# Eight routed experts in a different order, with a form for 32 tokens and a scatter in four steps

## The reference

```
def _moe(h, router_w, router_b, wg, wu, wd):
    logits = (h @ router_w + router_b).astype(jnp.float32)
    top_v, top_i = lax.top_k(logits, MOE_TOPK)
    top_w = jax.nn.softmax(top_v, axis=-1)
    gates = jnp.sum(top_w[..., None] * jax.nn.one_hot(top_i, N_EXPERTS, dtype=jnp.float32), axis=-2)
    ...
    for e in range(N_EXPERTS):
        out = out + gates[..., e:e + 1] * _swiglu(h, wg[e], wu[e], wd[e])
```

## Time and profile before

| | us |
|---|---|
| median of 3 runs | 2050.29 (2046.76 to 2052.06) |
| the profiled execution | 2052.97 |
| its span in the profile | 2051.2 |
| TensorE busy | 1945.4 (95% of the span) |
| VectorE, ScalarE, GpSimd busy | 501.9, 276.1, 351.3 |
| first product of the experts to the last | 1053.9 to 2028.4 |

### The profile page before, as it was taken

How to read it: one execution, slowest core, us unless ns; L and a number is a source line. 1 busy time by engine, 2 the same in 40 slices (tenths; PEclk the granted TensorE clock), 3 DMA queues, 4 the chain that set the end, 5 groups by cost and what they waited for, 6 DMA issues and landing times.

```text
span 2051.2 us, 28236 instructions
## 1 busy us (share of the span) xinstructions
PE 1945.4 (95%) x11415; PEld 1379.9 (67%) x11416; DVE 501.9 (24%) x1098; ACT 276.1 (13%) x519; POOL 351.3 (17%) x215
## 2 busy tenths in 40 slices
PE   7999799989999999999979999998988999999998
PEld 5888588867776788888855555554446877554444
DVE  1794734110001391434130101110101100101102
ACT  2104212010001203412020001010000000101002
POOL 2609900079993000000000000000000000000000
PEclk9999899999999999999979999999999999999999
DMA  9746433267773343333479999999999666799840
GB/s 381 256 152 226 164 124 122 85 241 258 269 274 147 121 163 131 117 110 123 174 305 401 420 417 352 417 422 422 422 422 420 241 245 246 308 382 421 311 179 22
DMA packets 73841, 533.82 MB, mean 260 GB/s; under 512 B 8320, under 2 KB 8320, under 8 KB 8960
## 3 DMA queue, kind: packets, MB, share of 16 engines
q1 hardware_dynamic: 67680, 489.72, 60.8%
q0 software_dynamic: 5760, 41.95, 5.6%
q10 hardware_dynamic: 288, 0.50, 0.1%
HBM read 531.08 MB, written 1.05 MB: 259 GB/s over the span
## 4 chain that ended last, share of the span: by engine, by line
PE 84%; SPq 4%; DMA 4%; DVE 4%; ACT 2%; issue 2%; POOL 1%; ACTq 0%; DVEq 0%
PE ps L614 21%; PE ps L953 17%; PE ps L988 9%; PE ps L677 7%; PE ps L686 7%; PE ps L1017 6%; SPq L449 4%; PE ps L697 4%; PE ps L1033 3%; PE ps L912 2%; PE ps L929 2%; DMA ring<-in_moe_units 1%; DMA xc<-in_moe_units 1%; DMA proj<-in_ada_units 1%; PE ps L973 1%
## 5 line engine op out<-in xcount | busy, mean ns | idle before, releaser
L614 PE MATMUL ps<-hT,ring 128*128 128x256 f32 x2048 | 454.4, 383 | 5.0 <-ACT hT L1136 5.0
L614 PEld LDWEIGHTS ps<-hT,ring 128*128 128x128 f32 x2048 | 390.9, 192 | 61.0 <-issue 8.3
L953 PE MATMUL ps<-ring,proj 128*64 128x256 f32 (+2 forms) x1768 | 204.7, 369 | 7.9 <-DMA ring<-in_moe_units 7.9
L534 POOL TENSOR_TENSOR aring<-aring,ccol 128x2048 f32<-128x2048 f32 x40 | 145.0, 3624 | 236.6 <-ACT hT L1136 162.8
L953 PEld LDWEIGHTS ps<-ring,proj 128*64 128x64 f32 (+2 forms) x1768 | 119.6, 134 | 86.1 <-issue 41.0
L1663 DVE TENSOR_TENSOR proj<-proj,ps 128x256 f32<-128x256 f32 (+2 forms) x49 | 23.4, 479 | 616.5 <-PE ps L953 616.5
L686 PE MATMUL ps<-hT,ring 128*128 128x256 f32 x704 | 156.8, 385 | 4.0 <-ACT hT L1136 4.0
L686 PEld LDWEIGHTS ps<-hT,ring 128*128 128x128 f32 x704 | 135.4, 194 | 22.5 <-issue 4.4
L540 POOL TENSOR_TENSOR aring<-aring 128x1024 f32<-128x1024 f32 x80 | 149.4, 1867 | 6.3
L1466 DVE SCALAR_TENSOR_TENSOR misc<-cpad,par,misc 128x256 f32<-128x256 f32 x240 | 102.7, 511 | 0.0
L1259 ACT ACTIVATE proj<-ps 128x256 f32<-128x256 f32 (+2 forms) x49 | 21.0, 429 | 590.6 <-PE ps L953 590.6
(11 more groups left out here) (291 smaller groups left out, 2042.0 us busy)
## 6 DMA issues: line engine op xcount, KB each, us to landing
ring<-in_moe_units SPq DMA_DIRECT2D x144, 1024.0 KB, 14.1
ring<-in_dense_units SPq DMA_DIRECT2D x121, 1024.0 KB, 5.0
aring<-in_moe_units SPq DMA_DIRECT2D x48, 1024.0 KB, 12.7
proj<-in_moe_units SPq DMA_DIRECT2D x48, 1024.0 KB, 16.1
aring<-in_ada_units POOLq DMA_DIRECT2D x40, 1024.0 KB, 6.2
extra<-in_moe_units SPq DMA_DIRECT2D x24, 1024.0 KB, 12.8
xc<-in_moe_units SPq DMA_DIRECT2D x24, 1024.0 KB, 16.3
misc<-in_moe_units SPq DMA_DIRECT2D x24, 1024.0 KB, 18.3
```

Source lines behind the costliest of these rows:

```text
L534: last = g.tensor_tensor(w, w, ccol[:, :].unsqueeze(2).broadcast_to([P, KT, 256]), ALU.mult)
L614: last = mm(ps[:, n % 2, j * SEQ:(j + 1) * SEQ], wide(s)[:, k, j * P:(j + 1) * P], hT[:, k, :], start=(k == 0), stop=(k == KT - 1))
L953: last = mm(ps[rows * c:rows * (c + 1), bank, 4 * t0:4 * (t0 + rows)], xg[:, 4 * h + k, t0:t0 + rows], w[:, k, 4 * rows * c:4 * rows * (c ...
```

## The change

1. VectorE ranks experts 1 to 7 by their count on the chip and permutes the counts, `key9` and `gate9` accordingly. With r the rank (0 for most tokens), the place among the seven is min(2r, 13 - 2r). Expert 0 stays first. For the counts above the order is 0, 5, 6, 7, 3, 1, 2, 4, with 24, 153, 20, 128, 30, 67, 41 and 49 tokens.
2. SP reads from the new tensor `turn` which expert's weights to load: it waits for `ord_s`, which VectorE gives when the order is made, before unit 14 of the first expert, and reads two entries at the start of each pass.
3. There is a body for up to 32 tokens (`quarter_rows`). Gate and up products have a 32-token stationary operand in four column quarters, each of which sums two of the eight slices of the width 1024 for all 512 columns. ScalarE and VectorE copy the partial sums out, and `sum_and_turn` adds the four quarters and transposes in one, by products with `stk` (four stacked 32x32 identities). Then come silu on ScalarE, the product on VectorE, and the down product in four quarters.
4. The scatter is done in four steps, in groups 1 to 4, each behind a branch of its own (`by_rows`: 64, 128 or 256 rows). A step makes two of the eight tiles, one in bank 6 and one in bank 7. Up to 64 tokens its two products have 64 rows, one in each row half of the array. In `quarter_rows` the two halves of the inner sum lie in rows 0 to 31 and 32 to 63 and are added by the same product.

```diff
-SIZES = (HALF, 96, 128, 160, 256)
+SIZES = (QUARTER, HALF, 96, 128, 160, 256)
...
+        def by_rows(eng, count, body):
+
+            with eng.If(count <= HALF):
+                body(HALF)
+            with eng.Else():
+                with eng.If(count <= P):
+                    body(P)
+                with eng.Else():
+                    body(SEQ)
+                eng.nop()
+
         def count_after(eng, e):
+            eng.wait_ge(ord_s, 1)
             return eng.value_load(cnt[0:1, ds(e + 2, 1)], min_val=0, max_val=SEQ)
...
                 expert_load(0, u)
+            def expert_of(place):
+                return sp.value_load(turn[0:1, place], min_val=0, max_val=EXPERTS - 1)
+
+            sp.wait_ge(ord_s, 1)
             with sp.Fori(0, EXPERTS - 1) as e:
+                now, following = expert_of(ds(e, 1)), expert_of(ds(e + 1, 1))
                 for u in range(EXP_SLOTS, UNITS):
                     sp.wait_ge(unit_s, e * UNITS + (u - EXP_SLOTS + 1))
-                    expert_load(e, u)
+                    expert_load(now, u)
                 for u in range(EXP_SLOTS):
                     sp.wait_ge(unit_s, e * UNITS + (UNITS + u - EXP_SLOTS + 1))
-                    expert_load(e + 1, u)
+                    expert_load(following, u)
+            final = expert_of(slice(EXPERTS - 1, EXPERTS))
             for u in range(EXP_SLOTS, UNITS):
                 sp.wait_ge(unit_s, (EXPERTS - 1) * UNITS + u - EXP_SLOTS + 1)
-                expert_load(EXPERTS - 1, u)
+                expert_load(final, u)
...
+            def scatter(n, step, free_at):
+
+                pe.wait_ge(cf_s, free_at + 2 * step)
+                for c in range(2):
+                    m = step + 4 * c
+                    if n == HALF:
+                        r0 = HALF * c
+                        mm(ps[:, 6 + c, 0:SEQ], ysb[r0:r0 + HALF, 0, step * P:(step + 1) * P], pgT[r0:r0 + HALF, 0, :],
+                           start=True, stop=True).then_inc(c_s, 1)
+                        continue
+                    for st in range(n // P):
+                        last = mm(ps[:, 6 + c, 0:SEQ], ysb[:, st, m * P:(m + 1) * P], pgT[:, st, :],
+                                  start=(st == 0), stop=(st == n // P - 1))
                     last.then_inc(c_s, 1)
...
-                            scatter_before()
+                        if 1 <= g <= 4:
+                            scatter_before(g - 1)
...
+                    def product(kind, g, bank):
+                        for h in range(2):
+                            w = cols4(arrived((kind, g, h)))
+                            for k in range(4):
+                                last = mm(ps[n * k:n * (k + 1), bank, :], xg[:, 4 * h + k, 0:n], w[:, k, :],
+                                          start=(h == 0), stop=(h == 1))
+                            last.then_inc(unit_s, 1)
+
+                    def gate(g):
+                        if g:
+                            pe.wait_ge(esil_s, S0 + g)
...
+                    def sum_and_turn(g):
+                        pe.wait_ge(esil_s, S0 + g + 1)
+                        pe.wait_ge(ehm_s, S0 + g + 1)
+                        for part, c0 in ((silx, 0), (hst, P)):
+                            for j in range(4):
+                                last = mm(ps[:, 4 + g % 2, c0 + j * n:c0 + (j + 1) * n],
+                                          part[:, g % 2, j * P:(j + 1) * P], stk[:, :], start=True, stop=True)
+                        last.then_inc(eht_s, 1)
+
+                    def down_quarter(g):
+                        pe.wait_ge(ehte_s, S0 + g + 1)
+                        for h in range(2):
+                            w = rows1(arrived(("d", g, h)))
+                            for i in range(2):
+                                for c in range(2):
+                                    r0 = n * (2 * c + i)
+                                    last = mm(ps[r0:r0 + n, 2, :], hmt[:, g % 2, (2 * h + i) * n:(2 * h + i + 1) * n],
+                                              w[:, i, 512 * c:512 * (c + 1)],
+                                              start=(g == 0 and h == 0), stop=(g == GE - 1 and h == 1))
+                            last.then_inc(unit_s, 1)
+
+                    pe.wait_ge(stk_s, 1)
+                    gate(0)
+                    up(0)
+                    for g in range(1, GE):
+                        gate(g)
+                        sum_and_turn(g - 1)
+                        up(g)
+                        if g == 1:
+                            after = count_after(pe, e)
+                        if 1 <= g <= 4:
+                            scatter_before(g - 1)
+                        down_quarter(g - 1)
+                    sum_and_turn(GE - 1)
...
+                def scatter_before(step):
 
                     pe.wait_ge(ye_s, e + 1)
-                    by_size(pe, before, lambda slots: scatter(slots, e * PER + CF0 + C1 - 1))
+                    by_rows(pe, before, lambda rows: scatter(rows, step, e * PER + CF0 + C1))
...
+            def scatter_last(rows):
+                for step in range(4):
+                    scatter(rows, step, PER * EXPERTS + CF0 + C1)
+
+            by_rows(pe, last_count, scatter_last)
...
+                def part_copy(g):
+                    act.wait_ge(unit_s, E0 + AT["g", g, 1] + 1)
+                    if g >= 2:
+                        act.wait_ge(eht_s, S0 + g - 1)
+                    a_(silx[:, g % 2, :], ps[:, 0, :], ACT.Copy).then_inc(esil_s, 1)
+
+                def quarter_silu(g):
+                    act.wait_ge(eht_s, S0 + g + 1)
+                    a_(hmt[:, g % 2, 512:512 + P], ps[:, 4 + g % 2, 0:P], ACT.Silu).then_inc(qsil_s, 1)
+
+                if n == QUARTER:
+                    part_copy(0)
+                    for g in range(1, GE):
+                        part_copy(g)
+                        quarter_silu(g - 1)
+                        if g == 1:
+                            after = count_after(act, e)
+                    quarter_silu(GE - 1)
+                    act.sem_inc(wsil_s, 4 * GE)
...
-                evac_y(n)
+                if n <= HALF:
+                    a_(ysb[:, 0, 0:512], ps[:, 2, :], ACT.Copy).then_inc(ye_s, 1)
+                else:
+                    evac_y(n)
...
+            then_wait(v.tensor_tensor(R[17], R[13], R[14], ALU.add))
+            v.tensor_copy(gate9[:, :, 0:1], rt[:, 17, :, 0:1])
+
+            then_wait(v.scalar_tensor_tensor(order_c[:, 1, :], order_c[:, 0, :], float(EXPERTS), slot_f[:, 0:EXPERTS],
+                                             ALU.mult, ALU.subtract))
+            weight = order_c[:, 1, 1:EXPERTS]
+            square = [P, OTHERS, OTHERS]
+            then_wait(v.tensor_tensor(order_m, weight.unsqueeze(1).broadcast_to(square),
+                                      weight.unsqueeze(2).broadcast_to(square), ALU.is_gt))
+            rank, place = order_c[:, 2, 0:OTHERS], order_c[:, 3, 0:OTHERS]
+            then_wait(v.tensor_reduce(rank, order_m, AX.X, ALU.add))
+            then_wait(v.tensor_scalar(place, rank, -2.0, 2.0 * OTHERS - 1.0, ALU.mult, ALU.add))
+            then_wait(v.scalar_tensor_tensor(place, rank, 2.0, place, ALU.mult, ALU.min))
+            then_wait(v.tensor_tensor(order_m, slot_f[:, 0:OTHERS].unsqueeze(2).broadcast_to(square),
+                                      place.unsqueeze(1).broadcast_to(square), ALU.is_equal))
+
+            def placed(values, dst):
+
+                then_wait(v.tensor_tensor(order_t, order_m, values.unsqueeze(1).broadcast_to(square), ALU.mult))
+                then_wait(v.tensor_reduce(dst, order_t, AX.X, ALU.add))
+
+            placed(order_c[:, 0, 1:EXPERTS], order_c[:, 4, 0:OTHERS])
+            placed(slot_f[:, 1:EXPERTS], order_c[:, 5, 1:EXPERTS])
+            v.memset(order_c[:, 5, 0:1], 0.0)
+            for t in range(TT):
+                placed(rt[:, 15, t, 1:EXPERTS], order_c[:, 6, 0:OTHERS])
+                v.tensor_scalar(key9[:, t, 1:EXPERTS], order_c[:, 6, 0:OTHERS], -1.0, None, ALU.add)
+                placed(rt[:, 17, t, 1:EXPERTS], gate9[:, t, 1:EXPERTS])
+            v.tensor_copy(cnt[0:1, 2:EXPERTS + 1], order_c[0:1, 4, 0:OTHERS])
+            v.tensor_copy(turn[:, :], order_c[0:1, 5, :]).then_inc(ord_s, 1)
...
+            def merge(step, products):
+
+                for c in range(2):
+                    m = step + 4 * c
+                    dve.wait_ge(c_s, products + 2 * step + c + 1)
+                    v.scalar_tensor_tensor(xT[:, m, :], ps[:, 6 + c, 0:SEQ], modc[:, 40 + m:41 + m],
                                            xT[:, m, :], ALU.mult, ALU.add).then_inc(cf_s, 1)
...
+                        if 1 <= g <= 4:
+                            merge(g - 1, e * PER + C1)
                         if g == 1:
-                            merge_before()
                             after = count_after(dve, e)
...
+                    def part_copy(g):
```

(11 more changed lines are left out.)

89 lines of the change are left out of this document (61 added, 28 removed).

## The result

The changed kernel takes **2034.47 us** (median of 4 runs, 2032.68 to 2037.89) against 2049.28 (2046.76 to 2052.06) before: ratio 0.993, 95% interval [0.992, 0.994]. It is faster, by 15 us. The forecast was 2001 with a range of 1989 to 2019: the sign was right, the time was not, by 33 us. The profiled execution took 2033.62 us, its span 2031.9.

The account below looks back on a forecast made before the run. Two limits take turns: weight loads bound small experts, TensorE large ones while the full ring stops loads. Experts end at 1978.7, plus tail 23.0 makes 2001.7; plus 1.8 less 2.7 gives 2001 us, range 1989 to 2019.

Parts of the forecast that it names:

- Expert 5: 160-token body, second in order: 203.7 us including 3.69 of issue, 1 us less than before by scatter; ends at 1343.9.
- Expert 7: 128-token body, fourth in order: 163.7 us with 3.72 of issue, less 1, plus 0.6 to the next expert; 1586.0.
- the last four: Experts 3, 1, 2, 4: loads never stop, 392.7 us at 2.485 per unit, 9 more than TensorE's 383.4.
- the ring is large enough: Weight buffer of 14 units: expert 1 consumes 28 us slower than the loads, 11 units, so loads go on.
- Entering a body is dear each time: Rival: experts 6, 3, 1 and 2 also pay 3.7 us at entry, giving 2007; chance 0.13.
- Expert 0: First expert, 32-token body: first new load about 1061 after the order code, end at 1140.2 against 1142.9 before.
- The tail: After the last expert: 23.0 us against 22.8, last scatter 6.8 instead of 5.95, one copy of y less, 0.6.
- Expert 6: 32-token body behind a full ring, third in order: 78.8 us, where the old body would take 91.
- The 32-token body: Products 1.8 us each, `sum_and_turn` 2.0, group 7.4 against 10.86; a body of 64 instead would give back 22.
- The scatter's worth: Four steps let merges fall beside products: 4 us instead of about 5 in expert 5; 1 less in expert 7.
- The branches of the scatter: Rival: four branches per expert stall TensorE; gain gone at 2.9 us each, 2066 at 3.7; chance 0.04.
- The order's worth: New order of experts, large ones filling the ring ahead of small ones: 27 us of the gain by itself.

Follow-up runs that it names:

- Run 4: Changed kernel with the code of the 64-token body placed ahead of the 32-token body, last comparison turned to fit: 2021.23 us.
- run 1: Changed kernel with its eight experts written out in the order the chip makes for this input, no loop or dispatch: 2003.0 us.
- run 9: Changed kernel with all four scatter steps in group 1 under one branch, instead of spread over groups 1 to 4: 2050.72 us.
- run 12: Changed kernel with experts written out, and the 64-token body in place of the 32-token one: 2008.03 us.
- runs 3: Changed kernel without the 32-token body, keeping the order and the four-step scatter: 2025.3 us.
- run 11: Kernel before with the new order alone, keeping its own bodies and its own scatter in one place: 2037.31 us.
- run 10: Changed kernel with the experts left in order 0 to 7, ordering instructions still present: 2060.89 us.
- the written-out pair: Kernel before and changed kernel, each with its experts written out in its own order, without loop or dispatch: 2041.65 and 2003.0 us.
- the hinted one: Changed kernel with a dispatch in each body and a TensorE prefetch hint for the next body just ahead of the last gather: 2014.84 us.

## Why the prediction was wrong, step by step

**The step that failed** is the costing of the entries: "Expert 5" and "Expert 7" with their old 3.69 and 3.72 us, and the last four with none, "the ring is large enough", 9 us of slack. The rival "Entering a body is dear each time" had the mechanism, with a chance of 0.13, and was too small: 2007. It put 3.7 on each entry by the earlier trace rows; they are 5.5 to 6.0. The misses are no longer than before, but the 3.7 was what they left behind a 64-token body, and behind the new, shorter one 5.5 to 5.7 is left. The prediction priced the wait and not what covered it. It took the 64-token body as one "placed early" and so cheap, and 64 behind 64 as free, by the earlier trace rows; but the 0.62 there was the price of the *first* body, and the diff put another body first. Run 4 shows this by itself: the same code with 64 first is 13.2 us quicker. And it let the DMA hide the rest, which holds only while the ring isn't full.

The 31.5 us between runs of the changed kernel and of run 1, in their two profiles (33.1 us of span): 22.3 of stalls are in the last three entries alone, 12.0 in those before. They don't add up to the loss, since small experts that wait for loads hide a part. By windows (each ends behind the entry into the next expert), places 1 to 5 lose 19.8, places 6 and 7 22.4, the last one wins 13.7 back from its full ring; 1.5 is at the start and 3.1 in the tail. Two costs come on top of the stall. After it the granted clock is low. The stretch behind the entry into expert 1, in the changed kernel and in run 1 (the last three columns are clock, DMA share and GB/s):

```profile
1678.10:1684.00 5.90, 5.89 (x32) 3.41 (x32) 0.00 (x0) 0.00 (x0) 0.00 (x0) 0.56 1.01 418
```

```profile
1656.80:1662.00 5.20, 5.20 (x94) 3.77 (x94) 0.00 (x0) 0.60 (x1) 0.00 (x0) 1.00 1.00 411
```

So for some 6 us TensorE ran near the lower of its two levels, 1.2 instead of 2.4 GHz, and the 288 products that open the expert took 19.07 us against 16.46 in run 1. And the loads stop, 244 instead of 408 GB/s.

**Expert 0:** ends at 1142.4, forecast 1140.2. The first load goes at 1060.82, forecast 1061; the order code is no cost beyond that. **Expert 5** up to its last product: 1148.00 to 1346.15 is 198.2, forecast 203.7 less 3.69, or 200.0. **Expert 6:** 80.5 from 1347.0 to 1427.5, forecast 78.8. **Expert 7:** 163.3 with its entry of 5.49, forecast 163.3 with entries of 3.72 and 0.6. That the two agree is luck: without entries it is 157.8, forecast 159.0. **The last four:** 413.6 to 2004.4, forecast 392.7; with no entries 399.0, so 6 of the 21 were not the entries: the loads ran at 416 to 419 GB/s with short gaps, not at 422. **The tail:** 27.5, forecast 23.0, and 24.4 with the experts written out. The chain there:

```profile
2006.11 1.98 issue
2008.09 1.24 PE ps L956 x3
...
2009.35 0.49 DVE xT L1798
...
2009.89 1.27 PE ps L956 x4
```

An issue wait of 1.98 us stands inside the first step; that it is a fetch isn't shown. And a step is 2.2 us, not 1.7: the products of a step were costed at 0.4 and take 1.2. The granted clock is 0.51 from 2009 to 2018; in run 9 the same four records take 0.70 in the first two steps of the last scatter and 1.22 in the last two.

**The 32-token body's durations were right.** The chain of the changed kernel in expert 3 (a product of the program is two records, so x16 is eight products):

```profile
1596.10 1.90 PE ps L1065 x16
1598.00 1.85 PE ps L1046 x16
1599.85 1.06 PE ps L960 x4
1600.91 1.85 PE ps L1076 x16
1602.77 1.72 PE ps L1046 x16
```

Forecast 1.8 a product, 2.0 for `sum_and_turn` (L1065) and about 1.0 for a scatter step (L960; the 64-row pair is 0.63): right within 0.15. **Its worth was wrong,** 5.0 and not 22. Written out, expert 6 takes 89.2 with the 64-token body (forecast 91) and 84.1 with the 32-token one (forecast 78.8), so 5.1 and not 12. In the latter the last load that the gather has to wait for lands 71 us into the expert, forecast 69, and from 1405 to 1412 the granted clock is 0.50 after TensorE has waited for loads: `sum_and_turn` takes 3.55 us there instead of 1.90. For expert 0 the forecast had 10 us; it ends at 1142.3 in run 12 and at 1140.8 in run 1, so 1.5. The 4.6 us that the 64-token form was to wait for VectorE didn't come: it is busy 87.1 of its 88.9 us.

**The scatter's worth was wrong the other way:** forecast some 2 us, measured 11 on the order alone (runs 3 and 11) and 16 net by run 9. About 1 us a step is the merge that no longer lies on the path, in every expert: 12.0 us of waits in run 11, 19.6 in run 9. Of run 9's 16, 3.29 is a stall that has nothing to do with the merges, and it has 10.78 less at the entries. **The branches of the scatter** don't stall: at the scatter products of the expert stage TensorE waits 0.2 us of issue in all. That rival is out. **The order's worth** of 27 is met by run 10 (26.4), but not by run 11 (14.5): what the order can give depends on what the body changes cost, and the written-out pair gives most, 2041.65 to 2003.0.

So the forecast's 2001 stood for a kernel without dispatch, which takes 2003.0, and even there it is near by luck. Against the span of run 1, 1998.8, it counts 8.0 us of entries that run 1 doesn't have, and experts 5 and 7 apart from them are 5.1 and 3.4 too long; expert 6 is 5.3 too short, the last four 6.3 and the tail 1.4. Both later versions beat the two kernels and keep the order on the chip: 64 placed first, 2021.2, and the hinted one, 2014.8.

## What to carry to other kernels

When a change adds a body of code or moves one, cost every entry, not the ones that the old order had: a cheap entry in the old profile may be the price of the place right behind the dispatch, which only one body can have. Ask also what the engine still holds when the branch comes: the same miss of 6 us cost 3.7 behind a body of long products, 5.6 behind one of short products, and a miss of 4.2 cost nothing behind the 128-token body. A body made shorter makes the next entry dearer. Put the body that is entered most where a wait would hurt first, and measure a version with the code written out in one order: the difference is what the dispatch costs. And a slack that depends on a buffer ahead of the engine is gone as soon as the engine stalls long enough to fill it.
